# The last projection's block sums and low parts on VectorE, its chains turned, and its last steps by 256 tokens

## What is computed

```
u_val, u_gate = split(depthwise_conv_seq(h2 @ w_up))        # 2 x 2816 columns
x = x + gate2 * ((gelu(u_gate) * u_val) @ w_down)           # [1024, 2816] @ [2816, 1024]
return rmsnorm(x, g_final)
```

## Time and profile before

| | |
|---|---|
| median of the runs | 2191.67 us |
| profiled execution | 2191.61 us |
| its span in the trace | 2189.8 us |
| TensorE busy | 2090.0 us, 95% |
| VectorE busy | 1355.3 us, 62% |
| GpSimd busy | 1295.0 us, 59% |
| ScalarE busy | 821.1 us, 37% |
| chain that ended last | TensorE 69%, VectorE 21%, ScalarE 3% |
| first and last matmul start of the last projection | 1936.0 and 2177.4 us |

### The profile page before, as it was taken

How to read it: one execution, slowest core, us unless ns; L and a number is a source line. 1 busy time by engine, 2 the same in 40 slices (tenths; PEclk the granted TensorE clock), 3 DMA queues, 4 the chain that set the end, 5 groups by cost and what they waited for, 6 DMA issues and landing times.

```text
span 2189.8 us, 28448 instructions
## 1 busy us (share of the span) xinstructions
PE 2090.0 (95%) x11124; PEld 1635.0 (75%) x11124; DVE 1355.3 (62%) x1614; ACT 821.1 (37%) x1304; POOL 1295.0 (59%) x884
## 2 busy tenths in 40 slices
PE   8999999999998999999999999998999999999897
PEld 5878746878876885578767788786788888877676
DVE  7999955631866115500168216867766666678987
ACT  6222242330126016610273442145455544443333
POOL 2575813067873654347556754473788888846773
PEclk9999999999999999999999999999999999999999
DMA  7463381042224220011221235323122222165433
GB/s 300 151 131 106 94 195 57 1 187 93 89 98 148 68 87 18 28 39 58 56 47 58 103 111 200 128 75 125 40 86 87 87 87 87 58 231 188 145 134 120
DMA packets 72725, 230.02 MB, mean 105 GB/s; under 512 B 15959, under 2 KB 18823, under 8 KB 71279
## 3 DMA queue, kind: packets, MB, share of 16 engines
q1 hardware_dynamic: 59632, 170.04, 23.6%
q10 hardware_dynamic: 9104, 36.45, 4.5%
q0 software_dynamic: 3856, 21.70, 3.8%
HBM read 180.03 MB, written 46.17 MB: 103 GB/s over the span
## 4 chain that ended last, share of the span: by engine, by line
PE 69%; DVE 21%; ACT 3%; issue 2%; POOL 2%; DMA 2%; SPq 1%; ACTq 0%; DVEq 0%
PE ps L3575 22%; PE ps L3173 17%; DVE back L2373 6%; PE ps L3499 4%; PE ps L3608 3%; DVE ffn_parts L2961 3%; PE ps L3690 3%; PE ps L3138 3%; PE ps L3646 2%; PE ps L354 2%; PE ps L524 1%; PE ps L512 1%; PE ps L377 1%; PE ps L506 1%; DVE h_high L2455 1%
## 5 line engine op out<-in xcount | busy, mean ns | idle before, releaser
L3690 PE MATMUL ps<-ffn_parts,w_parts 128*128 128x512 f32 x924 | 222.0, 400 | 17.3 <-DVE front L3011 7.2
L1776 POOL TENSOR_TENSOR up_parts<-front,up_parts 128x512 fp32r<-128x512 f32 x120 | 194.5, 1628 | 69.6 <-ACT up_parts L2106 69.5
L3690 PEld LDWEIGHTS ps<-ffn_parts,w_parts 128*128 128x128 f32 x924 | 175.6, 192 | 63.0 <-POOL w_parts L1804 16.0
L3575 PE MATMUL ps<-t_high,up_parts 128*128 128x512 f32 x640 | 204.9, 391 | 4.9 <-ACT back L2113 4.9
L1701 POOL TENSOR_TENSOR w_parts<-front,sb_zero 128x1024 fp32r<-128x1024 f32 x48 | 100.7, 2099 | 158.4 <-PE ps L3499 58.3
L3173 PE MATMUL ps<-h_high,w_parts 128*128 128x512 f32 x672 | 187.6, 394 | 0.6 <-PE ps L3499 0.6
L3575 PE MATMUL ps<-h_high,up_parts 128*128 128x512 f32 x480 | 154.5, 389 | 0.1
L1706 POOL TENSOR_TENSOR w_parts<-front,w_parts 128x1024 fp32r<-128x1024 f32 x54 | 141.9, 2628 | 21.3 <-ACT w_parts L2273 7.5
L3575 PEld LDWEIGHTS ps<-t_high,up_parts 128*128 128x128 f32 x640 | 121.0, 189 | 31.0 <-issue 5.7
L3173 PEld LDWEIGHTS ps<-h_high,w_parts 128*128 128x128 f32 x672 | 124.0, 188 | 25.8 <-issue 1.4
L1587 POOL TENSOR_TENSOR front<-front,sb_csilu 128x1024 f32<-128x1024 f32 x48 | 102.6, 2138 | 61.5 <-DMA front<-w_ada 61.4
(11 more groups left out here) (448 smaller groups left out, 5109.6 us busy)
## 6 DMA issues: line engine op xcount, KB each, us to landing
front<-w_ada SPq DMA_DIRECT2D x48, 512.0 KB, 3.6
front<-w_up SPq DMA_DIRECT2D x44, 512.0 KB, 4.2
front<-w_down SPq DMA_DIRECT2D x22, 512.0 KB, 3.7
back<-w_down SPq DMA_DIRECT2D x22, 512.0 KB, 4.5
front<-w_in SPq DMA_DIRECT2D x16, 512.0 KB, 4.0
front<-w_out SPq DMA_DIRECT2D x16, 512.0 KB, 4.5
residual<-back ACTq DMA_DIRECT2D x2, 4096.0 KB, 14.9
front<-w_gates SPq DMA_DIRECT2D x16, 512.0 KB, 4.4
```

The lines of the kernel that those rows point to most:

```text
L1776: pool.tensor_tensor(parts[:, BANK:], src, parts[:, 0:BANK].bitcast(F32), ALU.subtract)\
L3575: mm = pe.matmul(o, parts[:, at + k * P:at + (k + 1) * P], x, start=p in (1, 2, 5) and k == 0 and q == 0, stop=k == 3 and q == 2, skip_gro ...
L3690: mm = pe.matmul(ps[:, (4 if p in (2, 5, 3) else 0) + m, :], weights[:, w_ * BANK + m * P:w_ * BANK + (m + 1) * P], half_of(x, x_), start= ...
```

## The change

GpSimd makes the low parts of the weights of the first 8 steps (`POOL_STEPS`) only, and nothing after them; VectorE makes the low parts of the other 69 and also the 22 sums s2. t2 is written over t1. In turns 0 to 2 the order of the two products of a pair is changed so that the chain that the next turn needs first ends one step before the other, and the drain of the second is put behind one more `down_low`. All t4 move from turn 1 to turn 3. At the start of the stage two `down_low` come ahead of t1 and t3, and the sums of three pairs follow together. The last four steps run first for tokens 0 to 255, then for 256 to 511, with 256-wide matmuls, and the norm has three parts: tokens 512 to 1023, 0 to 255 and 256 to 511.

```diff
-        FINAL_HALVES = (1, 0)
+        FINAL_PARTS = ((BANK, BANK), (0, BANK // 2), (BANK // 2, BANK // 2))
+        FINAL_SUM = [ps[:, 4, 2 * P:3 * P], ps[:, 5, 2 * P:2 * P + 64], ps[:, 0, 2 * P:2 * P + 64]]
+        FINAL_SPREAD = [ps[:, 4:8, 0:P], ps[:, 4:8, 3 * P:3 * P + 64], ps[:, 0:4, 0:64]]
...
             return ACTV[:, (16 + at) % 6, :] if at < 6 else page(ACT_BACK[at - 6])
         DOWN_PAIRS = N_UP // 2
-        DOWN_STEPS = [(1, 0), (1, 1), (2, 0), (2, 1)] + [(p, j) for j in range(2, DOWN_PAIRS) for p in (1, 2)] + \
-            [(p, j) for two_ in ((6, 5), (7, 3)) for j in range(DOWN_PAIRS) for p in two_] + [(4, j) for j in range(DOWN_PAIRS)]
+        DOWN_STEPS = [(1, 0), (1, 1), (2, 0), (2, 1)] + [(p, j) for j in range(2, DOWN_PAIRS) for p in (2, 1)] + \
+            [(p, j) for j in range(DOWN_PAIRS) for p in (5, 6)] + [(p, j) for j in range(DOWN_PAIRS - 1) for p in (3, 7)] + \
+            [(7, DOWN_PAIRS - 1), (3, DOWN_PAIRS - 1)] + [(4, j) for j in range(DOWN_PAIRS)]
-        DOWN_LAST = (2, 5, 3, 4)
+        DOWN_LAST = ((1, 2), (5, 6), (3, 7), (4,))
+        POOL_STEPS = 8
+        def down_split(s):
+            if s < POOL_STEPS:
+                return S("w_split"), nth(B_DOWN) + s + 1
+            return S("block_sum"), UP.sums + 2 * (N_UP - FIRST) + s - POOL_STEPS + 1
-            return nth(B_DOWN) + DOWN_AT[DOWN_LAST[turn], j] + 1
+            return down_split(max(DOWN_AT[p, j] for p in DOWN_LAST[turn]))
...
-            def down_weight_low(s):
+            for s in range(POOL_STEPS):
                 high = W_DOWN[s % 4]
-            def down_sum_2(j):
-                s1, a11 = down_weights(5, j), down_weights(6, j)
-                pool.wait_ge(S("block_dve"), DOWN_DVE["s1", j])
-                pool.tensor_tensor(a11, s1, a11, ALU.subtract).then_inc(S("block_sum"), 1)
-            def down_sum_2_later(j):
-                s3, a22 = down_weights(7, j), half_of(down_second(down_load(7, j)), 1)
-                pool.wait_ge(S("block_dve"), DOWN_DVE["s3", j])
-                pool.tensor_tensor(a22, a22, s3, ALU.subtract).then_inc(S("block_sum"), 1)
-            for s in range(N_STEPS):
-                p, j = DOWN_STEPS[s]
-                if (p, j) == (2, DOWN_PAIRS - 1):
-                    down_sum_2(0)
-                elif p == 5:
-                    down_sum_2(j + 1) if j + 1 < DOWN_PAIRS else down_sum_2_later(0)
-                elif p == 3 and j + 1 < DOWN_PAIRS:
-                    down_sum_2_later(j + 1)
-                down_weight_low(s)
...
-                elif (p, j) == (4, 7):
+                elif (p, j) == (4, 6):
                     final_root_act(act, 0)
-            for q in range(12, 16):
-                final_square_act(act, q)
-            final_root_act(act, 1)
+            for i in (1, 2):
+                for q in range(4):
+                    final_square_act(act, 8 + 4 * i + q)
+                final_root_act(act, i)
...
+            def down_weight_low(s):
+                high = W_DOWN[s % 4]
+                dve.wait_ge(S("w_high"), down_high_done(s))
+                dve.tensor_tensor(half_of(high, 1), down_weights(*DOWN_STEPS[s]), half_of(high, 0).bitcast(F32), ALU.subtract)\
+                    .then_inc(S("block_sum"), 1)
             def down_low(s):
                 high = A_DOWN[s % 4]
+                if s >= POOL_STEPS:
+                    down_weight_low(s)
                 dve.wait_ge(S("ffn_high"), s + 1)
                 dve.tensor_tensor(half_of(high, 1), down_input(*DOWN_STEPS[s]), half_of(high, 0).bitcast(F32), ALU.subtract)\
                     .then_inc(S("ffn_split"), 1)
+            def down_t1_t3(j):
+                b11, b12, _, b22 = down_pair(j)
+                dve.wait_ge(S("ffn_split"), DOWN_AT[1, j] + 1)
+                down_sum("t1", j, b11, b12, b11, ALU.subtract)
+                down_sum("t3", j, b12, b22, b12, ALU.subtract, "t1")
             def down_t2(j):
                 t1, _, _, b22 = down_pair(j)
+                dve.wait_ge(S("ffn_split"), DOWN_AT[5, j] + 1)
+                down_sum("t2", j, t1, b22, t1, ALU.subtract)
             def down_t4(j):
-                b21 = down_pair(j)[2]
+                t2, _, b21, _ = down_pair(j)
+                down_sum("t4", j, b21, b21, t2, ALU.subtract, "t2")
+            def down_s1_s2(j):
+                d = down_load(5, j)
+                a11, s1 = half_of(down_first(d), 0), half_of(down_first(d), 1)
+                a21, a22 = half_of(down_second(d), 0), half_of(down_second(d), 1)
+                dve.wait_ge(*down_landed(d))
+                down_sum("s1", j, s1, a21, a22, ALU.add)
+                down_sum("s2", j, a11, s1, a11, ALU.subtract, "s1")
+            def down_s3_s2(j):
+                d = down_load(7, j)
+                a11, a21, a22 = half_of(down_first(d), 0), half_of(down_second(d), 0), half_of(down_second(d), 1)
+                dve.wait_ge(*down_landed(d))
+                down_sum("s3", j, a11, a11, a21, ALU.subtract)
+                down_sum("s2_later", j, a22, a22, a11, ALU.subtract, "s3")
...
-            down_t1(0)
-            down_t3(0)
             for j in range(2, DOWN_PAIRS):
-                last = j == DOWN_PAIRS - 1
+                down_low(DOWN_AT[2, j])
+                if j == DOWN_PAIRS - 1:
+                    down_s1_s2(0)
                 down_low(DOWN_AT[1, j])
-                if not last:
-                    down_low(DOWN_AT[2, j])
-                down_t1(j - 1)
-                down_t3(j - 1)
-                if last:
-                    down_s1(0)
-                    down_t2(0)
-                    down_low(DOWN_AT[2, j])
-            down_t1(DOWN_PAIRS - 1)
-            down_t3(DOWN_PAIRS - 1)
+                for i in range(3) if j == 2 else (j,):
+                    down_t1_t3(i)
             for j in range(DOWN_PAIRS):
                 if j == 1:
                     dve.wait_ge(S("back"), 48)
-                    down_out(DOWN_AT[1, DOWN_PAIRS - 1] + 1, 0, 0, 0, 0)
+                    down_out(DOWN_AT[2, DOWN_PAIRS - 1] + 1, 4, 0, 0, 0)
+                down_low(DOWN_AT[5, j])
+                if j == 1:
+                    down_out(DOWN_AT[1, DOWN_PAIRS - 1] + 1, 0, 0, 0, 1)
+                down_t2(j)
+                if j + 1 < DOWN_PAIRS:
+                    down_s1_s2(j + 1)
+                else:
+                    down_s3_s2(0)
+                    down_s4(0)
                 down_low(DOWN_AT[6, j])
-                down_t4(j)
                 if 4 <= j < 7:
                     final_add_dve(dve, j - 3)
             for j in range(DOWN_PAIRS):
-                if j == 1:
-                    down_out(DOWN_AT[6, DOWN_PAIRS - 1] + 1, 0, 0, 1, 0)
-                down_low(DOWN_AT[7, j])
                 if j == 1:
                     dve.wait_ge(S("landed3"), BACK_FROM[3] + 48)
                     down_out(DOWN_AT[5, DOWN_PAIRS - 1] + 1, 4, 1, 1, 0)
+                first, second = sorted(DOWN_AT[p, j] for p in (3, 7))
+                down_low(first)
+                if j == 1:
+                    down_out(DOWN_AT[6, DOWN_PAIRS - 1] + 1, 0, 0, 1, 0)
                 if j + 1 < DOWN_PAIRS:
-                    down_s3(j + 1)
-                down_low(DOWN_AT[3, j])
-                if j + 1 < DOWN_PAIRS:
+                    down_s3_s2(j + 1)
                     down_s4(j + 1)
+                else:
+                    down_t4(0)
+                down_low(second)
             for j in range(DOWN_PAIRS):
                 if j == 2:
-                    down_out(DOWN_AT[7, DOWN_PAIRS - 1] + 1, 0, 1, 1, 13)
+                    down_out(DOWN_AT[7, DOWN_PAIRS - 1] + 1, 0, 1, 1, 9)
                 elif j == 3:
-                    down_out(DOWN_AT[3, DOWN_PAIRS - 1] + 1, 4, 0, 1, 9)
-                elif j == 9:
+                elif j == 8:
                     final_rstd_dve(dve, 0)
                 down_low(DOWN_AT[4, j])
+                if j + 1 < DOWN_PAIRS:
+                    down_t4(j + 1)
+            def down_last(i, m):
+                a, n = FINAL_PARTS[i]
+                dve.wait_ge(S("down_used"), N_STEPS - 4 + 4 * (i - 1) + m + 1)
+                x = X4[:, 4 + m, a:a + n]
+                dve.scalar_tensor_tensor(x, ps[:, m, a:a + n], ada[:, 44 + m:45 + m], x,
+                                         ALU.mult, ALU.add).then_inc(S("x4_ready"), 1)
+            for k in range(4):
+                final_scale_dve(dve, 0, k)
+            for m in range(4):
+                down_last(1, m)
+                final_scale_dve(dve, 0, 4 + m)
+            final_rstd_dve(dve, 1)
+            for m in range(3):
+                down_last(2, m)
             for k in range(FT):
-                final_scale_dve(dve, 0, k)
-            down_out(N_STEPS - 3, 0, 1, 0, 0)
-            final_rstd_dve(dve, 1)
+                if k == 6:
+                    down_last(2, 3)
+                final_scale_dve(dve, 1, k)
+            final_rstd_dve(dve, 2)
             for k in range(FT):
```

(51 more changed lines are left out.)

99 lines of the change are left out of this document (40 added, 59 removed).

## The result

| | before | after |
|---|---|---|
| median of the runs | 2191.10 us (4: 2190.49 to 2192.22) | 2168.69 us (4: 2167.41 to 2170.93) |
| ratio, with its 95% interval | | 0.9898 [0.9881, 0.9915] |
| profiled execution, its span | 2191.61, 2189.8 us | 2167.41, 2165.6 us |
| first matmul of the last projection | 1936.04 | 1935.66 |
| **stage**: from there to the span's end | 253.8 us | 229.9 us |

The change takes 22.4 us off, 1.0%; predicted were 23.6 us and 2168.0. The 23.6 us were counted from the profiled execution, 2191.61. The row of the stage is the yardstick for all that follows. The code ahead of the last projection is the same in all these kernels, yet the stage began anywhere from 1934.2 to 1938.8 us in the executions that were profiled, which is more than most of the effects in question.

The account below looks back on a forecast made before the run. VectorE and GpSimd, waiting for each other, were taken to hold turns 1 and 2 above TensorE's pace. Start 2.4, turn 1 14.0, turn 2 8.3, end -1.1 sum to 23.6 us off 2191.61: 2168.0, range 2160 to 2177.

Parts of the forecast that it names:

- VectorE's price without GpSimd: Turns 1 and 2: 0.60 to 0.72 us an instruction, 4.44 us a pair, below TensorE's 5.44; saves 22.3 us.
- T: End of step 64, where turn 3's clock starts; at 2139.9 us before, predicted at 2115.2 us.
- Rival 1: Turns 1 and 2: VectorE's chain sets the pace after all, 5.84 us a pair, 2177 us; chance 0.15.
- rival 4: VectorE instructions stay long without GpSimd, 1.34 us each, 9.4 us a pair, some 2262 us; chance 0.03.
- The new wait ahead of step 6: Start, turn 0: six sums delay step 6's low part; a 2.2 us stall replaces the 2.69 us gap.
- Rival 2: TensorE is never late: no start stall (2.2), low parts in time (3.7), full clock (1.6); 2160.5 us; chance 0.12.
- Turn 3's schedule: Three VectorE instructions a step: 0.6 us stall at step 71, last low part at T+28.1, 3.7 us lost.
- 256-wide matmuls: Last four steps: 96 matmuls starting 0.12 us apart take 11.5 us for 10.9, +0.6.
- Rival 3: Last four steps: a 256-wide matmul also costs its weights' time, +6.7 us, 2175 us; chance 0.03.
- The lower clock in the last part: Last four steps: after near four idle us the clock may be lower for a while; 1.6 us taken.
- The tail: Behind the last matmul: about 9.5 us, 12.0 before; span's end at T+51.0.
- The turned chains: Turn starts: opening bank group now complete one step (2.72 us) early, so drains cause no stall, 0.9 us to spare.

Follow-up runs that it names:

- pool_lows: Changed kernel with all 77 low parts of the weights on GpSimd again, s2 still on VectorE; 2189.81 us, ratio to the kernel before 0.9996.
- t_later: Changed kernel with the sums t1 and t3 of the first five pairs spread behind steps 5, 7 and 9; 2167.18 us, ratio to the kernel before 0.9895.
- t4_early: Changed kernel with t4 made in turn 1 again; 2168.06 us, ratio to the kernel before 0.9902.
- again: Changed kernel run once more without an edit, as the yardstick of one chip; 2169.82 us, ratio to the kernel before 0.9910.
- only_move: Kernel before with only the weights' low parts from step 8 on and s2 moved to VectorE; 2168.30 us, ratio to the kernel before 0.9907.
- the two at 223: Changed kernel with spread sums and t4 over turns 1 and 2; one with earlier last drain, 2160.79 us, one with the old undivided tail, 2159.16 us.

## Why the prediction was right, and where it wasn't

- **VectorE's price without GpSimd: right.** Low parts at 0.68 to 0.69 us, 0.60 apart (0.72 behind a dependence); turns 1 and 2 at TensorE's pace. From the stage's start to T, 203.9 us became 179.5 (2139.9 - 1936.0 and 2115.2 - 1935.7): 24.4 saved, predicted 24.7 (start 2.4, turns 22.3). That T itself came at 2115.2 to the tenth is luck: the stage began 0.4 us earlier and took 0.3 us longer to T than worked out. By terms: the first six steps and their gap take 18.76 us, 2.44 over 16.32, for 4.6 before: 2.2 saved; the turns 22.2. A turn's pair took 4.46 us of VectorE for 4.44. Rival 1 (5.84 us a pair) and rival 4 (slow without GpSimd) fall with it. That GpSimd is the cause, and not the sum of instructions, pool_lows shows: with 69 instructions taken off VectorE again the stage is 23 us longer. Some 14 of them are waits in TensorE's timeline beyond those of the changed kernel, 7 the lower clock behind waits, and the rest is in pieces too small to tell. How much of the move is needed was not tried: there is no run between 8 and 77 steps on GpSimd.
- **The new wait ahead of step 6: right**, 2.27 us for 2.2, by the chain given, and t_later shows that the sums ahead of the low part are the cause. Rival 2 falls here.
- **Turn 3's schedule: right.** The wait ahead of step 71 0.87 for 0.6; last low part at T+28.1, the very term of the sum; from the first of the last part's first 72 matmuls to the last one's end 12.3 us for 8.9 at their spacing, so 3.4 lost for 3.7. t4_early shows what made them late: t4 in turn 3. Without it 0.45 us of waits were left there.
- **256-wide matmuls: right**, (7.79 - 0.28) / 62 = 0.121 us apart for 0.12. Rival 3 falls.
- **The lower clock in the last part (1.6 us): half right.** Not in the profiled execution, but in again and t_later (1.5 us each), and the last part of pool_lows took 9.88 us at 0.76. The prediction took as certain what comes in some executions.
- **The tail: too short by 0.6 us.** The term "that gives 9.5 us behind the last matmul" measured 10.1. The spread took 0.70 us for 0.4 (0.45 in again and t_later), and it was 3.0 us from the last scale to the span's end for 2.6. The drain's lateness, 0.8 us, was in the sum. The two errors of the end, the clock that wasn't paid (1.6 too much) and the tail (0.6 too little), partly take each other out: T+50.4 for T+51.0. That the end came so close is in part luck.
- **The turned chains: my reading was wrong, though no number hung on it.** I wrote that now the bank group that opens the next turn is complete a step early, as if that were new. In the kernel before each new turn already opened with the group finished first; its gaps of 2.91 and 4.08 us came from VectorE's backlog. only_move keeps the old order and has 0.86 and 0.70 us there. The waits that the turned order can have removed are at most these 1.6 us, bought with t4 in turn 3 (0.87 and 2.8 us of waits). Even that is not shown to be the order's doing: t4_early has the turned order with t4 in turn 1, as only_move has it, and waits 1.44 and 0.85 us at the start of turn 2.
- **Where the gain sits.** I summed the parts of the change as if each had its share. The runs give 23.0 of the stage's 23.9 us to the move. What the rest brings up to T (5.4 us, 3.1 of them in turn 0) turn 3 and the tail take back but for about 1, which is less than two profiles of one kernel differ.
- **Two small things.** The prediction set the 0.60 us between VectorE's starts against the Trainium skill, VectorE: DVE Perf Modes, section The DRAIN you can't avoid. That section adds that a next op that is not held starts earlier, so the independent instructions at 0.60 us don't contradict it. And rival 4's 2262 is 2264 by its own terms; no chance hung on it.

What stays open: how large a part of the move would have been enough, why the stage's start moves by some 4 us between executions of unchanged code, and what decides whether the clock drops in the last part. The differences between the kernels of 228.7 to 232.3 us rest on one profiled execution each; their medians are within 2.6 us of each other. Only the two at 223 and pool_lows at 252.9 stand apart.

## What to carry to other kernels

Where two engines both show long instructions of one kind while they run side by side, and short ones when the other pauses, count the work at the short price on one of them alone; if that is under the pace of the bound engine, move it there. Here the sums without the 69 low parts brought nothing (pool_lows), and with them 23 us; amounts between were not run. Then count not the average pair but each pair with all that is added to it (drains, adds, sums ahead), and spread the extras over pairs that have room: that was worth 7 us of stage here (222.8 for 229.9), and about 8 us of time (ratio to the kernel before 0.9860 for 0.9898). A wait also costs what the clock takes behind it: 6.8 us in pool_lows. A tail cut in finer parts is worth what the last part's latency shrinks by, less what the added sums and spreads cost and what the earlier parts put in its way; here nothing was left.

## What the runs showed of the hardware that I had not expected

- GpSimd's low parts on 128x512 lengthen VectorE's so much that 69 instructions less on VectorE go with a stage 23 us longer: its low parts take 1.10 us in the mean (pool_lows) against 0.74, and those on GpSimd 1.54.
- Waits of 4.68 and 3.46 us on TensorE (pool_lows) were followed by stretches at a granted clock of 0.74 (1960 to 1965 us) and 0.50 (2070 to 2075 us); 0.50 is the lower of the two levels, 1.2 GHz, all through. Of two waits of like length at the start, 2.69 us in the kernel before was followed by 0.66 (1950 to 1955 us) and 2.67 us in again by 1.00 (1955 to 1960 us).
- A granted clock of 0.83 between 2140 and 2150 us in two executions and of 1.00 in a third, the matmuls of that stretch being the same, each time behind the same two waits of 1.40 us (after, again, t_later).
